# Retention values of heads 1 to 3: seven block products in place of the full product

## The reference

```python
proj = h @ w_in
q = rotary(proj[..., :dq].reshape(bsz, seq, B_HEADS, B_DK))
k = rotary(proj[..., dq:2 * dq].reshape(bsz, seq, B_HEADS, B_DK)) * (B_DK ** -0.5)
v = proj[..., 2 * dq:2 * dq + dv].reshape(bsz, seq, B_HEADS, B_DV)
g = proj[..., 2 * dq + dv:]
...
ret = (intra + cross).reshape(bsz, seq, B_HEADS, B_DV)
ret = rms_norm(ret, out_g)
y = ret * silu(g)
return y @ w_out
```

## Time and profile before

| | us |
|---|---|
| median of three runs | 2100.87 |
| profiled execution | 2100.51 |
| its span | 2098.7 |
| TensorE busy | 2079.6 (99%) |
| VectorE busy | 1436.8 (68%) |
| GpSimd busy | 1213.0 (58%) |
| ScalarE busy | 1135.1 (54%) |

### The profile page before, as it was taken

How to read it: one execution, slowest core, us unless ns; L and a number is a source line. 1 busy time by engine, 2 the same in 40 slices (tenths; PEclk the granted TensorE clock), 3 DMA queues, 4 the chain that set the end, 5 groups by cost and what they waited for, 6 DMA issues and landing times.

```text
span 2098.7 us, 31298 instructions
## 1 busy us (share of the span) xinstructions
PE 2079.6 (99%) x11739; PEld 1815.0 (86%) x11739; DVE 1436.8 (68%) x2363; ACT 1135.1 (54%) x1874; POOL 1213.0 (58%) x757
## 2 busy tenths in 40 slices
PE   9999999999999999999999999999999999999999
PEld 7867889889898989888899898888887888899998
DVE  7973886767586666776776684897577325885773
ACT  6564654654553536456646544446877435645642
POOL 3514666874686657645658844655433554838843
PEclk9999999999999999999999999999999999999999
DMA  4203233333323132232233325322222243333232
GB/s 168 71 11 96 94 94 101 101 101 109 117 62 116 62 105 77 94 98 91 91 101 105 107 89 182 101 81 81 71 62 70 95 138 91 101 101 101 91 109 93
DMA packets 57685, 200.79 MB, mean 96 GB/s; under 512 B 6400, under 2 KB 7168, under 8 KB 57280
## 3 DMA queue, kind: packets, MB, share of 16 engines
q1 hardware_dynamic: 56816, 197.46, 29.7%
q10 hardware_dynamic: 720, 1.34, 0.2%
HBM read 194.32 MB, written 4.19 MB: 95 GB/s over the span
## 4 chain that ended last, share of the span: by engine, by line
PE 58%; DVE 2%; ACT 1%; issue 1%; ACTq 0%; DVEq 0%
PE ps L421 13%; PE ps L422 13%; PE ps L423 13%; PE ps L724 5%; PE ps L726 5%; PE ps L725 5%; PE ps L451 1%; PE ps L449 1%; PE ps L450 1%; PE ps L2789 1%; PE ps L2774 0%; PE ps L2801 0%; DVE G L1851 0%; PE ps L2776 0%; PE ps L2798 0%
## 5 line engine op out<-in xcount | busy, mean ns | idle before, releaser
L399 POOL TENSOR_TENSOR WL<-WS,WH 128x1024 fp32r<-128x1024 f32 (+1 forms) x248 | 586.6, 2369 | 537.8 <-ACT WH L389 537.2
L421 PE MATMUL ps<-H,WH 128*128 128x512 f32 (+2 forms) x1264 | 493.0, 390 | 2.3 <-DVE H L629 1.8
L422 PE MATMUL ps<-H,WH 128*128 128x512 f32 (+2 forms) x1264 | 490.7, 388 | 0.0
L423 PE MATMUL ps<-H,WL 128*128 128x512 f32 (+2 forms) x1264 | 490.5, 388 | 0.0
L1236 POOL TENSOR_TENSOR WL<-WS,WH 128x512 fp32r<-128x512 f32 x232 | 311.8, 1357 | 243.2 <-ACT WH L847 241.7
L389 ACT ACTIVATE WH<-WS 128x1024 fp32r<-128x1024 f32 (+2 forms) x250 | 256.9, 1030 | 169.9 <-PE ps L423 87.9
L421 PEld LDWEIGHTS ps<-H,WH 128*128 128x128 f32 (+1 forms) x1264 | 237.0, 188 | 52.0 <-issue 3.1
L423 PEld LDWEIGHTS ps<-H,WL 128*128 128x128 f32 (+1 forms) x1264 | 236.9, 187 | 49.4
L422 PEld LDWEIGHTS ps<-H,WH 128*128 128x128 f32 (+1 forms) x1264 | 237.1, 188 | 46.2
L421 PE MATMUL ps<-G,WH 128*128 128x512 f32 x496 | 193.8, 391 | 2.8 <-DVE G L2508 1.4
L422 PE MATMUL ps<-G,WH 128*128 128x512 f32 x496 | 193.1, 389 | 0.0
(11 more groups left out here) (378 smaller groups left out, 4811.8 us busy)
## 6 DMA issues: line engine op xcount, KB each, us to landing
WS<-in_w SPq DMA_DIRECT2D x337, 512.0 KB, 3.5
WS<-in_w SPq DMA_DIRECT2D x24, 384.0 KB, 3.0
xs<-X SPq DMA_DIRECT2D x1, 2048.0 KB, 6.9
X<-xs SPq DMA_DIRECT2D x8, 256.0 KB, 3.7
out<-X SPq DMA_DIRECT2D x8, 256.0 KB, 2.0
X<-in_sg SPq DMA_DIRECT2D x1, 1344.0 KB, 5.8
X<-in_x ACTq DMA_DIRECT2D x4, 256.0 KB, 5.8
X<-in_x SPq DMA_DIRECT2D x4, 256.0 KB, 5.5
```

Of the source, the lines that this page charges most:

```text
L399: e.tensor_tensor(lo, raw, hi.bitcast(F), ALU.subtract).then_inc(*P.sig("w_lo", i))
L421: e.matmul(out, lh, rh, start=start, stop=False)
L422: e.matmul(out, lh, rl, start=False, stop=False)
L423: return e.matmul(out, ll, rh, start=False, stop=stop)
```

## The change

The values of heads 1 to 3 are made as a paired unit of a new kind, `rv`. Head 0 stays as it was. The four DMA units of a head hold now the blocks a11, a21, a22, a12 (output half by odd or even input block, 1024 columns each), and `pe_value_pair` runs seven products for each of two 128-token blocks: tokens are on the output's partitions, so the halves of the tokens are what the t forms combine.

```diff
-PAIRED_UNITS = ("dns", "ups", "rp")
+PAIRED_UNITS = ("dns", "ups", "rp", "rv")
...
+    if key[0] == "rv":
+        return [[("w_lo", (key[0:2], "a11")), ("r_sum", (key[0:2], "s3"))], [("r_sum", (key[0:2], "low s3"))],
+                [("w_lo", (key[0:2], "a22"))], [("w_lo", (key[0:2], "a12")), ("r_sum", (key[0:2], "s4"))]][second]
...
+V_ORDER = ("a11", "s1", "s2", "s4", "s3", "a22", "a12")
...
+def pe_value_pair(P, e, h):
...
+    o = [bank(P, e, (("bv", h), j), True) for j in range(4)]
+    for name in V_ORDER:
+        cells(P, (pair, name), 2)
+    def product(name, b, out, first, ready=None):
...
+        if b == 0:
+            e.wait_ge(*P.at(*(("r_sum", (pair, "low " + name)) if name in ("s3", "s4") else ("w_lo", key))))
+        for q in range(4):
...
+            w = slice(256 * q, 256 * q + 256)
+            e.matmul(out, rh, hi[:, w], start=first and q == 0, stop=False, skip_group_check=True)
+            e.matmul(out, rh, lo[:, w], start=False, stop=False, skip_group_check=True)
+            t = e.matmul(out, rl, hi[:, w], start=False, stop=q == 3, skip_group_check=True)
...
+    for b in range(2):
+        product("a11", b, chain[b], True)
+    for b in range(2):
+        product("s1", b, right[b], True)
+    for b in range(2):
+        product("s2", b, chain[b], False, ("ct", (pair, "p1", b)))
+    for b in range(2):
+        product("s4", b, right[b], False, ("ct", (pair, "p5", b)))
+    for b in range(2):
+        product("s3", b, chain[b], False, ("ct", (pair, "u2", b)))
+    for b in range(2):
+        product("a22", b, chain[b], False, ("c22", (pair, b)))
+        product("a12", b, left[b], False)
```

ScalarE makes the first three forms at the end of the head before, behind the output units' casts, and the other four, with the copies of partial results, in the head:

```diff
# act_ret, in the head
+        if h in V_PAIRED:
+            value_part(h, "p1")
+            value_forms(h, "s4")
+            value_part(h, "p5")
+            value_forms(h, "s3")
+            value_part(h, "u2")
+            value_forms(h, "a22", "a12")
+            forms(one, "a11", "s1")
+            value(h, 2)
+            value(h, 3)
+            forms(one, "s2")
+            value(h, 0)
+            value(h, 1)
+            forms(one, "a12")
...
# act_ret, last lines of the loop over h
         for mp in range(1 if h == 2 else 4):
             cast(("bout", h, mp))
...
+        if h + 1 in V_PAIRED:
+            value_forms(h + 1, "a11", "s1", "s2")
```

VectorE makes the four sums of 1024 columns (`value_sum`), the low parts of the forms s3 and s4 (`value_sum_low`) and the additions that put the partial results together (`value_c`); GpSimd makes the other five low parts:

```diff
# dve_ret, in the head
+            value_sum(h, "s4")
+            value_sum(h, "s3")
+            value_sum_low(h, "s4")
+            value_sum_low(h, "s3")
+            value_c(h, "c12", 0)
+            value_c(h, "c12", 1)
+            value_c(h, "c22", 0)
+            e.wait_ge(*P.at("r_sum", (("rv", h), "low s4")))
+            sums(one, "s1")
+            value_c(h, "c22", 1)
...
# dve_ret, at the output units, behind turned(h + 1, 1)
         for mp in range(1 if h == 2 else 4):
+            if h + 1 in V_PAIRED and mp == (0 if h == 2 else 2):
+                value_sum(h + 1, "s1")
+            if h + 1 in V_PAIRED and mp == 3:
+                value_sum(h + 1, "s2")
...
+        if h == 2 and h + 1 in V_PAIRED:
+            value_sum(h + 1, "s2")
# pool_ret
+        if h in V_PAIRED:
+            for name in ("a11", "s1", "s2", "a22", "a12"):
...
+                e.wait_ge(*P.at("w_hi", key))
+                e.tensor_tensor(lo, v_raw(P, h, name) if name[0] == "a" else v_sum(P, h, name), hi.bitcast(F),
+                                ALU.subtract).then_inc(*P.sig("w_lo", key))
+        else:
+            units(("bv", h, 3))
```

More of the change, by code:

```diff
@@ L1400, in pe_row_pair, with v_raw, v_raw_in, v_sum @@
     P.cell_n += 1
+V_ORDER = ("a11", "s1", "s2", "s4", "s3", "a22", "a12")
+def v_raw(P, h, name):
+    i = P.index.get(("rv", h, ("a11", "a21", "a22", "a12").index(name)), 0)
+    return P.m["WS"][:, i % STAGE * NXW:i % STAGE * NXW + NXW]
+def v_raw_in(P, h, name):
+    i = P.index.get(("rv", h, ("a11", "a21", "a22", "a12").index(name)), 0)
+    return f"w_in{i % STAGE}", i
+def v_sum(P, h, name):
+    return {"s1": P.m["SQ"][:, 0:NXW], "s2": P.m["TMP"][:, 0:NXW], "s3": v_raw(P, h, "a21"), "s4": P.m["SQ"][:, 0:NXW]}[name]
@@ new lines, in v_part @@
+def v_part(P, name, b):
+    return r_sil(P, ("p1", "u2", "p5").index(name))[:, 256 * b:256 * b + 256]
+def pe_value_pair(P, e, h):
+    pair = ("rv", h)
+    for z in range(4):
+        listed(P, ("rv", h, z))
+    o = [bank(P, e, (("bv", h), j), True) for j in range(4)]
+    for name in V_ORDER:
+        cells(P, (pair, name), 2)
+    def product(name, b, out, first, ready=None):
+        key = (pair, name)
+        hi, lo = P.cell(key, NXW)
+        if ready:
+            e.wait_ge(*P.at(*ready))
+        if b == 0:
+            e.wait_ge(*P.at(*(("r_sum", (pair, "low " + name)) if name in ("s3", "s4") else ("w_lo", key))))
+        for q in range(4):
+            if name in ("a11", "a12", "s4"):
+                k, c = 2 * q + (name != "a11"), slice(256 * (name == "s4") + 128 * b, 256 * (name == "s4") + 128 * b + 128)
+                rh, rl = P.H(k, 0)[:, c], P.H(k, 1)[:, c]
+            else:
+                form, c = {"s1": "t1", "s2": "t2", "s3": "t3", "a22": "t4"}[name], slice(128 * b, 128 * b + 128)
+                rh, rl = r_tx(P, q, 0, form)[:, c], r_tx(P, q, 1, form)[:, c]
+            w = slice(256 * q, 256 * q + 256)
+            e.matmul(out, rh, hi[:, w], start=first and q == 0, stop=False, skip_group_check=True)
+            e.matmul(out, rh, lo[:, w], start=False, stop=False, skip_group_check=True)
+            t = e.matmul(out, rl, hi[:, w], start=False, stop=q == 3, skip_group_check=True)
+        t.then_inc(*P.sig("prod", (pair, name, b)))
+        P.end["cell", key] = ("prod", (pair, name, 1))
+    chain, left, right = [o[b][:, 256:512] for b in range(2)], [o[b][:, 0:256] for b in range(2)], [o[b + 2][:, 0:256] for b in range(2)]
+    for b in range(2):
[11 more added lines that the diff above has]
+        product("a12", b, left[b], False)
+    for j in range(4):
+        drop(P, (("bv", h), j))
@@ L1416, in pe_ret @@
     for h in range(4):
-        for _ in tokens(P, e, ("bv", h), [("bv", h, u) for u in range(4)]):
-            pass
+        if h in V_PAIRED:
+            pe_value_pair(P, e, h)
+        else:
+            for _ in tokens(P, e, ("bv", h), [("bv", h, u) for u in range(4)]):
+                pass
         for j in range(4):
@@ L1520, in part, with value_forms, value_part, value @@
         e.activation(dst, src, ACT.Copy).then_inc(*P.sig("ct", (pair, name)))
+    def value_forms(h, *names):
+        for name in names:
+            key = (("rv", h), name)
+            if name[0] == "a":
+                e.wait_ge(*P.at(*v_raw_in(P, h, name)))
+            else:
+                e.wait_ge(*P.at("r_sum", key))
+            for u in P.cell_before[key]:
+                e.wait_ge(*P.freed("cell", u))
+            e.activation(P.cell(key, NXW)[0], v_raw(P, h, name) if name[0] == "a" else v_sum(P, h, name),
+                         ACT.Copy).then_inc(*P.sig("w_hi", key))
+            if name == "a12":
+                P.hi_n = P.index.get(("rv", h, 3), 0) + 1
+    def value_part(h, name):
+        for b in range(2):
+            j, c, ready = {"p1": (b, slice(256, 512), "a11"), "p5": (b + 2, slice(0, 256), "s1"),
+                           "u2": (b, slice(256, 512), "s2")}[name]
+            e.wait_ge(*P.at("prod", (("rv", h), ready, b)))
+            e.activation(v_part(P, name, b), P.ps((("bv", h), j))[:, c], ACT.Copy).then_inc(*P.sig("ct", (("rv", h), name, b)))
+    def value(h, j):
+        if h in V_PAIRED:
+            e.wait_ge(*P.at(*(("c11", (("rv", h), j)) if j < 2 else ("c22", (("rv", h), j - 2)))))
+            if j >= 2:
+                e.wait_ge(*P.at("c12", (("rv", h), j - 2)))
+        else:
+            e.wait_ge(*P.at("tok", (("bv", h), 3, j)))
+        if h and j == 2:
+            e.wait_ge(*P.at("ret", (h - 1, 3)))
+        e.activation(r_v(P, j, 0), P.ps((("bv", h), j)), ACT.Copy).then_inc(*P.sig("v_hi", (h, j)))
     def decayed(h, j):
@@ L1553, in act_ret @@
         q, k = ("qk", 2 * h + 2), ("qk", 2 * h + 3)
-        cast(("bv", h, 0))
-        if h == 0:
+        if h in V_PAIRED:
+            value_part(h, "p1")
[11 more added lines that the diff above has]
+            forms(one, "a12")
+        else:
+            cast(("bv", h, 0))
             qk_split(0, 1)
             turned_hi(2)
-        cast(("bv", h, 1))
-        if h == 0:
+            cast(("bv", h, 1))
             turned_hi(3)
[L1561 to L1568, removed]
+            cast(("bv", h, 2))
+            cast(("bv", h, 3))
+            forms(one, "a11", "s1", "s2", "a12")
+            for j in range(4):
+                value(h, j)
         forms(one, "s3")
@@ L1721, in turned, with value_sum @@
                 *P.sig("qk_lo", (h, i)))
+    def value_sum(h, name):
+        key, dst = (("rv", h), name), v_sum(P, h, name)
+        a11, a12, a21, a22 = (v_raw(P, h, raw) for raw in ("a11", "a12", "a21", "a22"))
+        if name == "s1":
+            e.wait_ge(*P.at(*v_raw_in(P, h, "a21")))
```

(75 more changed lines are left out.)

5 lines of the change are left out of this document (4 added, 1 removed).

## The result

The changed kernel takes **2105.23 us** (median of 20 runs, 2104.46 to 2106.75) against 2100.77 before (20 runs, 2100.64 to 2102.46): ratio 1.0021, 95% interval 1.0014 to 1.0027. It is slower by 4.5 us. The profiled execution took 2104.67 us with a span of 2102.9, 4.2 us over the span of before.

The account below looks back on a forecast made before the run. TensorE was taken to bound the kernel, busy 2079.6 of 2098.7 us. Terms -4.9 + 6.65 + 0.4 + 1.0 = +3.15 us on 2100.51, plus 0.36 to the median, gave 2104.0 us; forecast band 2101.8 to 2105.0 (0.50), range 2100.0 to 2107.5.

Parts of the forecast that it names:

- the clock's term: Behind head 3's wait: TensorE's clock may fall to 1.2 GHz, costing 0 to 3.3 us; 1.0 us taken.
- the hidden 0.4 us: Head 3's values, behind the first wait: further waits for later forms, 0.4 us, between 0 and 1.3.
- The gain: Value stages on TensorE: 168 short matmuls take 20.12 us for 21.76, 1.64 us a head, 4.9 us for three.
- Heads 1 and 2 without a wait: Value stages of heads 1 and 2: every form is ready in time, so they keep their 3.3 us.
- The tightest chain: Heads 1 and 2: a12's form is ready at 15.3 us from stage start, wanted at 15.8, 0.5 us to spare.
- GpSimd's added work: Each paired head's values: five low parts instead of four, 2.40 us each, so +2.4 us a head.
- Head 3's wait: Before head 3's first value product: TensorE waits 6.65 us for a11's low part; upper bound 9.9 us.
- 4.0 us back: VectorE's rotation before head 3: two subtractions at 0.68 us each instead of 2.50 and 2.88, shortening the chain 4.0 us.
- The end of the chain: Head 3: a11's low part on GpSimd meets VectorE's sum and is ready at 852.9 rather than 852.15.
- the fall: Rival, head 3's first products after the wait: clock falls, costing 3.3 us, total 2105.9 us; chance 0.20.
- the bound of slower: Whole kernel: about 0.2% (4.2 us) tells from no change, so above 2105.1 us is slower; chance 0.35.
- my likeliest number: Whole kernel: forecast median of 2104.0 us.

Follow-up runs that it names:

- experiment 1: Changed kernel with only heads 1 and 2 paired, head 3 in the full product as before: 2097.66 us, ratio 0.9983.
- Experiment 5: Changed kernel plus two extra 1024-column GpSimd subtractions behind the output unit's low part ahead of head 3: 2108.95 us, ratio 1.0039.
- experiment 3: Changed kernel plus 27 extra 512-column matmuls ahead of head 3's first value product, adding no result: 2103.75 us, ratio 1.0012.
- experiment 6: Changed kernel with head 3's a11 high part moved on ScalarE ahead of both qk_split calls: 2106.1 us, ratio 1.0024.
- experiment 7: Changed kernel with head 3's whole preparation on ScalarE and VectorE reordered by need: 2103.96 us, ratio 1.0013.
- experiment 8: Experiment 7's kernel with ScalarE's qk_split calls and VectorE's additions and subtractions reordered against its three measured waits: 2098.21 us, ratio 0.9988.
- experiment 4: Changed kernel with 13 extra matmuls ahead of head 3's first value product, in place of experiment 3's 27: 2105.81 us, ratio 1.0022.

## Why the prediction was right

The sum was -4.9 + 6.65 + 0.4 + 1.0 = +3.15; measured between the two profiled executions were -4.8, +6.64, 0 and +1.64, with +0.7 of small pieces that it hadn't, +4.2 in all. The mechanism was the one forecast; the clock's term was mis-sized, the small pieces were missing, and the hidden 0.4 us, which the prediction names as possible and still counts in its sum, took a part of that back.

- *The gain.* Right: 20.15 us a stage for 20.12 predicted. The pace of a short matmul could be read from a gate pair.
- *Heads 1 and 2 without a wait.* Right; experiment 1 shows it by time as well. The tightest chain, a12 with 0.5 us to spare, held. GpSimd's added work was put too low, at 2.4 us a head, where its busy time grew by 17.4 for three: beside VectorE's operations its low parts took 3.05 and 3.36 us, not 2.40. It cost nothing there.
- *Head 3's wait.* Right in place, cause and size. It rested on two readings: that `hi_to` stops at a paired unit, so that a11's high part moves behind both `qk_split` calls, and that GpSimd's absence gives VectorE 4.0 us back. Experiment 5 puts these 4.0 back and finds them again. Without this step the forecast would have been 3.3 us too high. The rule of the Trainium skill on the shared port (SBUF — State Buffer, "SBUF: two separate sides") stands: this case's traces agree, with 2.50 and 2.89 us beside GpSimd's work and 0.68 without.
- *The end of the chain.* a11's low part met VectorE's sum and took 3.05 us, as taken. The 0.4 us of further waits didn't come, because the slow clock hid them; in experiment 3, without it, s1's low part was late by 0.37 us between starts.
- *The clock.* The mis-sized term. I took 1.0 of 0 to 3.3 as a guess, and gave the fall a chance of its own of 0.20. It did fall, and cost 1.64 us: the fall came in the course of the wait, where it is free, and only some 16 matmuls ran at the low level, 0.213 us apart in place of 0.120. The Trainium skill (TensorE: Matmul & The Clock Gate, "What's actually happening") says that an idle TensorE falls to 1.2 GHz; this case's trace agrees, with 0.50 behind the wait. I should have held the fall itself for likely and its price for small. That the trace of before showed 1.00 throughout was chance, of the one execution profiled (last section).

The median ended 4.5 us above before, just past the 4.2 us that I called the bound of slower, a case that had 0.35; my likeliest number lay 1.2 us below it, on the other side of that bound. Between the profiled executions the sum was 1.0 too low: the clock's 0.6, the small pieces' 0.7 and 0.1 of the gain, less the 0.4 us that the low clock hid. The medians lie another 0.2 apart.

## What to carry to other kernels

A change that takes matmul time off the bound must also be followed to its first product: look at how much other work of the bound stands ahead of it, and at which instruction of each helper's queue its inputs now stand. Where a helper stops at a new kind of unit, everything that it used to run ahead moves behind what was queued next. And a wait can cost more than its length, by the clock behind it and by the handovers. So changing three heads can be worth less than changing two.

## What else the runs showed of the hardware

The runs of one kernel fall into two groups some 1.6 us apart. Of the 31 runs of before beside experiments 1, 3, 6 and 7, 21 lie from 2100.5 to 2101.0 and 10 from 2101.9 up. Two profiles show what differs: near 117 us, in the attention block, TensorE waits for 1.43 us for GpSimd in both (first the kernel before, then experiment 8, whose profiled run took 2099.59 us, 1.4 over its median), and in one of them the clock falls.

```profile
116.00:118.00 2.00, 0.73 (x4) 0.25 (x2) 1.45 (x5) 0.50 (x1) 0.60 (x3) 1.00 0.01 4
118.00:120.00 2.00, 1.84 (x8) 1.16 (x9) 0.18 (x1) 1.97 (x5) 0.36 (x2) 1.00 0.00 0
```
```profile
116.00:118.00 2.00, 0.68 (x3) 0.20 (x2) 1.40 (x5) 0.55 (x1) 0.60 (x3) 1.00 0.02 4
118.00:120.00 2.00, 1.89 (x6) 1.40 (x7) 0.22 (x1) 1.97 (x5) 0.31 (x1) 0.50 0.00 0
```

The two programs are the same up to there. The next wait over 1 us ends 1.50 us later in the second:

```profile
159.56 0.50 PE L421 MATMUL ps<-G,WH 128*128 128x512 f32 x1 [1.41 <-DVE G L2508]
```
```profile
161.06 0.50 PE L431 MATMUL ps<-G,WH 128*128 128x512 f32 x1 [1.41 <-DVE G L2754]
```

The other profiles bear it out. In four of the eleven the granted clock from 118 to 120 us is 0.50 to 0.57 (experiments 3, 4, 6 and 8), and each of these four executions is one of the longer runs of its kernel; in the other seven it is 1.00, and none of them is. So a wait of 1.43 us in thin work brings the clock down in some executions and not in others, and a single profile may stand on either side of it. No run takes this wait away to see whether the two groups then merge.
